# QK-norm and rotary in a hybrid decoder step: norm weights folded into the rotation matrix, one root and one reciprocal for all 16 tiles, spread back by a matmul

## The reference, cut to what matters

```
def rmsnorm(x, g):
    y = x * lax.rsqrt(jnp.mean(x * x, axis=-1, keepdims=True) + RMS_EPS)
    return y * g
def rope(x, pos):            # per half of 64 channels: x1, x2 of 32 each
    return concatenate([x1 * cos - x2 * sin, x2 * cos + x1 * sin])
q = rope(rmsnorm(q.reshape(bsz, t, H_ATT, 2, DH), W["q_norm"][e]), pos)
k = rope(rmsnorm(k.reshape(bsz, t, H_ATT, 2, DH), W["k_norm"][e]), pos)
```

## Time and profile before

| | |
|---|---|
| median of 3 runs | 3424.6 us |
| the profiled execution's own time | 3428.04 us |
| its span | 3426.4 us |
| PE, DVE, ACT busy share of the span | 94%, 44%, 32% |
| the stage at issue: last copy of the projection to first attention matmul | 452.24 to 522.73 us |

### The profile page before, as it was taken

How to read it: one execution, slowest core, us unless ns; L and a number is a source line. 1 busy time by engine, 2 the same in 40 slices (tenths; PEclk the granted TensorE clock), 3 DMA queues, 4 the chain that set the end, 5 groups by cost and what they waited for, 6 DMA issues and landing times.

```text
span 3426.4 us, 56080 instructions
## 1 busy us (share of the span) xinstructions
PE 3235.2 (94%) x21279; PEld 2959.4 (86%) x21279; DVE 1520.3 (44%) x1994; ACT 1083.0 (32%) x1287; POOL 29.7 (1%) x55
## 2 busy tenths in 40 slices
PE   7899987997789999999999989999989999999998
PEld 2588853775778998998998989999989999999998
DVE  1534574113653443443433564445554444444443
ACT  1322233103333323323323333333343333333332
POOL 0000000000000000000000000000000000000000
PEclk8999996877899999999999989999999999999999
DMA  9777777662347557557567534444434444444443
GB/s 347 243 246 249 236 267 261 226 239 80 100 146 247 179 179 245 177 184 246 167 193 243 161 114 150 151 147 149 148 116 149 151 147 148 151 147 149 151 147 110
DMA packets 512217, 624.17 MB, mean 182 GB/s; under 512 B 22416, under 2 KB 408081, under 8 KB 511444
## 3 DMA queue, kind: packets, MB, share of 16 engines
q1 hardware_dynamic: 504576, 595.68, 54.5%
q0 software_dynamic: 6112, 22.84, 1.8%
q10 hardware_dynamic: 1430, 4.24, 0.4%
HBM read 617.13 MB, written 5.54 MB: 182 GB/s over the span
## 4 chain that ended last, share of the span: by engine, by line
PE 88%; DVE 4%; DMA 4%; ACT 1%; issue 1%; SPq 0%; POOL 0%; POOLq 0%; DVEq 0%; ACTq 0%
PE mm L1417 80%; PE aux L1417 7%; DMA wide_first<-in_ada_mix_w 2%; DMA vpage<-in_cache_v 2%; PE mm L1510 1%; DVE a_rr L1201 1%; DVE l_g L1308 0%; SPq L362 0%; ACT tmp L613 0%; DVE a_qn L1204 0%; DVE pj L1212 0%; DVE p_s L1228 0%; DVE a_t L1210 0%; DVE rstd L898 0%; DVE a_t L1208 0%
## 5 line engine op out<-in xcount | busy, mean ns | idle before, releaser
L844 DVE TENSOR_TENSOR w_lo<-raw,w_hi 128x1024 fp32r<-128x1024 f32 x752 | 920.2, 1226 | 1431.2 <-ACT w_hi L526 1429.4
L526 ACT ACTIVATE w_hi<-raw 128x1024 fp32r<-128x1024 f32 x752 | 795.4, 1059 | 1724.8 <-PE mm L1417 1724.8
L1417 PE MATMUL mm<-h_hi,w_hi 128*128 128x320 f32 x3712 | 1164.6, 314 | 54.2 <-DVE h_lo L940 32.3
L1417 PE MATMUL mm<-h_hi,w_lo 128*128 128x320 f32 x3712 | 1151.4, 310 | 0.0
L1417 PE MATMUL mm<-h_lo,w_hi 128*128 128x320 f32 x3712 | 1151.3, 310 | 0.0
L1417 PEld LDWEIGHTS mm<-h_hi,w_hi 128*128 128x128 f32 x3712 | 701.5, 189 | 135.8 <-issue 133.2
L1417 PE MATMUL mm<-u_hi,w_hi 128*128 128x320 f32 x2304 | 712.0, 309 | 0.0
L1417 PE MATMUL mm<-u_hi,w_lo 128*128 128x320 f32 x2304 | 711.9, 309 | 0.0
L1417 PE MATMUL mm<-u_lo,w_hi 128*128 128x320 f32 x2304 | 711.9, 309 | 0.0
L1417 PEld LDWEIGHTS mm<-h_lo,w_hi 128*128 128x128 f32 x3712 | 701.7, 189 | 2.2 <-issue 2.2
L1417 PEld LDWEIGHTS mm<-h_hi,w_lo 128*128 128x128 f32 x3712 | 701.1, 189 | 0.0
(11 more groups left out here) (247 smaller groups left out, 1448.2 us busy)
## 6 DMA issues: line engine op xcount, KB each, us to landing
raw<-in_mlp_w SPq DMA_DIRECT2D x512, 512.0 KB, 3.6
narrow<-in_ada_mlp_w SPq DMA_DIRECT2D x256, 256.0 KB, 3.6
raw<-in_w_in_odd SPq DMA_DIRECT2D x96, 512.0 KB, 3.6
raw<-in_w_in_even SPq DMA_DIRECT2D x80, 512.0 KB, 6.6
wide_first<-in_ada_mix_w SPq DMA_DIRECT2D x64, 512.0 KB, 8.8
narrow<-in_ada_mix_w SPq DMA_DIRECT2D x128, 256.0 KB, 3.7
wide_later<-in_ada_mlp_w SPq DMA_DIRECT2D x64, 512.0 KB, 6.0
wide_later<-in_ada_mix_w SPq DMA_DIRECT2D x64, 512.0 KB, 5.2
```

Source lines behind the costliest of these rows:

```text
L526: fn(w_hi[:, slot], raw[:, slot], ACT.Copy).then_inc(hi_ready, 1)
L844: v.tensor_tensor(w_lo[:, slot], raw[:, slot], w_hi[:, slot].bitcast(F32), ALU.subtract).then_inc(lo_ready, 1)
L1417: return nc.tensor.matmul(out, lhsT, rhs, start=first, stop=last)
```

## The change

- The norm weight no longer multiplies the tile. VectorE first makes `rot_g`, the rotation matrix with each row scaled by the norm weight of k or of q (two instructions). TensorE turns the raw tile with it; VectorE multiplies the raw tile by weight and cos in one instruction, the turned tile by sin, and adds both into `pj`. These sums are not normed yet.
- The sums of squares are gathered in one PSUM bank. `sel` has 32 columns for each group of four tiles, so that tile i adds its two sums as rows 2(i // 4) and 2(i // 4)+1 of the strip i % 4 of `mm[:, 1, 0]`.
- After the 16 tiles there is one root and one reciprocal over that bank. A second loop spreads each tile's two rows over the 128 partitions by a matmul with 32 rows of `bsel`, and VectorE multiplies the tile by it.
- The adaLN chunks come one at a time in both loops, where they came in pairs; the transposes of v lie in the first loop, those of k in the second, and two folds in each.
- The table of constants is 120 columns wider in sum; the mask of the sample attention is one window of 120 columns.

```diff
@@ -50,9 +50,9 @@
-for _name, _cols in (("ident", 128), ("halves", 128), ("rot", 128), ("ones", 128), ("comb", 64), ("fold", NC),
+for _name, _cols in (("ident", 128), ("sel", 128), ("bsel", 512), ("rot", 128), ("ones", 128), ("comb", 64), ("fold", NC),
-                     ("mask_s", NB * TS)):
+                     ("mask_s", 120)):
...
@@ -67,7 +67,14 @@
-    put("halves", (p[:, None] // DH == p[None, :] // DH))
+    sel = np.zeros((P, 4, 32))
+    bsel = np.zeros((P, 4, P))
+    for q in range(4):
+        for n in range(2):
+            sel[DH * n:DH * n + DH, q, 2 * q + n] = 1.0
+            bsel[2 * q + n::32, q, DH * n:DH * n + DH] = 1.0
+    put("sel", sel.reshape(P, 128))
+    put("bsel", bsel.reshape(P, 512))
...
@@ -95,11 +102,8 @@
-    t = np.arange(TS)
-    mask = np.full((NB, P, TS), NEG)
-    for b in range(NB):
-        mask[b] = np.where((t[None, :] // DS == b) & (t[None, :] % DS <= q % 8), 0.0, NEG)
-    put("mask_s", mask.transpose(1, 0, 2).reshape(P, NB * TS))
+    t = np.arange(120)[None, :] - 56
+    put("mask_s", np.where((t >= 0) & (t < DS) & (t <= q % 8), 0.0, NEG))
...
@@ -222,9 +226,9 @@
-        a_rt = at("a_rt", RH + 24576 + 2560, [P, 2, T])
-        a_rr = at("a_rr", RH + 24576 + 5120, [P, 2, T])
-        a_qn = at("a_qn", RH + 24576 + 7680, [P, 2, T])
+        a_rt = at("a_rt", RH + 24576 + 2560, [P, T])
+        a_rr = at("a_rr", RH + 24576 + 3840, [P, T])
+        rot_g = at("rot_g", RH + 24576 + 5120, [P, 2, P])
...
@@ -683,27 +688,29 @@
                     split(2)
             rounds(1)
             act.wait_ge(pair_free, 22)
-            for i in range(17):
-
-                if i < 16:
-                    if i >= 2:
-                        act.wait_ge(qk_ms, i - 1)
-                    fn(a_sq[:, i % 2], pj[:, qk_tile(i), :], ACT.Square).then_inc(qk_sq, 1)
-                if i >= 1:
-                    act.wait_ge(qk_ms, i)
-                    if i >= 3:
-                        act.wait_ge(qk_norm, i - 2)
-                    fn(a_rt[:, (i - 1) % 2], mm[:, 1, (i - 1) % 2, 0:T], ACT.Sqrt, scale=1.0 / DH, bias=C("eps")
-                       ).then_inc(qk_root, 1)
-                if i != 8:
-
-                    n = i if i < 8 else i - 1
-                    tok, cols = (vtok, ktok)[n // 8], slice((n % 8) * P, (n % 8) * P + P)
-                    act.wait_ge(tok_t, n + 1)
-                    fn(tok[:, 0:2, cols], tok_bank(n)[:, 0:2 * P].rearrange("p (a f) -> p a f", a=2), ACT.Copy)
-                    fn(tok[0:TS, 2, cols], tok_bank(n)[0:TS, 2 * P:3 * P], ACT.Copy).then_inc(tok_ready, 1)
-                if i % 4 == 3:
+            def tok_out(n):
+
+                tok, cols = (vtok, ktok)[n // 8], slice((n % 8) * P, (n % 8) * P + P)
+                act.wait_ge(tok_t, n + 1)
+                fn(tok[:, 0:2, cols], tok_bank(n)[:, 0:2 * P].rearrange("p (a f) -> p a f", a=2), ACT.Copy)
+                fn(tok[0:TS, 2, cols], tok_bank(n)[0:TS, 2 * P:3 * P], ACT.Copy).then_inc(tok_ready, 1)
+
+            for i in range(16):
+                if i >= 2:
+                    act.wait_ge(qk_ms, i - 1)
+                fn(a_sq[:, i % 2], pj[:, qk_tile(i), :], ACT.Square).then_inc(qk_sq, 1)
+                if i < 8:
+                    tok_out(i)
+                if i == 8:
                     ada_out(True)
+            act.wait_ge(qk_ms, 16)
+            fn(a_rt[:, :], mm[:, 1, 0, 0:T], ACT.Sqrt, scale=1.0 / DH, bias=C("eps")).then_inc(qk_root, 1)
+            ada_out(True)
+            for n in range(8, 16):
+                tok_out(n)
+                if n == 14:
+                    ada_out(True)
+            ada_out(True)
             for h in range(H + 1):
 
                 if h < H:
@@ -1196,28 +1203,30 @@
             dve.wait_ge(pair_free, G.now)
 
 
-            def qk_normed(i):
-                dve.wait_ge(qk_root, i + 1)
-                step(v.reciprocal(a_rr[:, i % 2], a_rt[:, i % 2]))
-                settle()
+            step(v.tensor_scalar(rot_g[:, 0], C("rot"), V("k_norm"), None, ALU.mult))
+            v.tensor_scalar(rot_g[:, 1], C("rot"), V("q_norm"), None, ALU.mult).then_inc(qk_gain, 1)
+            for i in range(16):
                 g = V("k_norm") if i < 8 else V("q_norm")
-                v.scalar_tensor_tensor(a_qn[:, i % 2], pj[:, qk_tile(i), :], g, a_rr[:, i % 2], ALU.mult, ALU.mult).then_inc(qk_norm, 1)
-
-            def qk_turned(i):
-                dve.wait_ge(qk_norm, i + 1)
-                step(v.tensor_tensor(a_t1[:, i % 2], a_qn[:, i % 2], C("cos"), ALU.mult))
+                x = pj[:, qk_tile(i), :]
+                step(v.scalar_tensor_tensor(a_t1[:, i % 2], x, g, C("cos"), ALU.mult, ALU.mult))
                 dve.wait_ge(qk_rot, i + 1)
                 step(v.tensor_tensor(a_t2[:, i % 2], mm[:, 0, i % 2, 0:T], C("sin"), ALU.mult))
                 settle()
-                v.tensor_tensor(pj[:, qk_tile(i), :], a_t1[:, i % 2], a_t2[:, i % 2], ALU.add).then_inc(qk_ready, 1)
-
-            for i in range(17):
-                if i < 16:
-                    qk_normed(i)
-                if i >= 1:
-                    qk_turned(i - 1)
-                if i % 4 == 0 and i:
-                    ada_bias(1, 3 + i // 4)
+                dve.wait_ge(qk_sq, i + 1)
+                v.tensor_tensor(x, a_t1[:, i % 2], a_t2[:, i % 2], ALU.add).then_inc(qk_part, 1)
+                if i == 9:
+                    ada_bias(1, 4)
+            dve.wait_ge(qk_root, 1)
+            v.reciprocal(a_rr[:, :], a_rt[:, :]).then_inc(qk_inv, 1)
+            ada_bias(1, 5)
+            dve.wait_ge(qk_part, 16)
+            for i in range(16):
+                x = pj[:, qk_tile(i), :]
+                dve.wait_ge(qk_spread, i + 1)
+                v.tensor_tensor(x, x, mm[:, 0, i % 2, 0:T], ALU.mult).then_inc(qk_ready, 1)
+                if i == 9:
+                    ada_bias(1, 6)
+            ada_bias(1, 7)
 
 
             def p_scores(h):
...
@@ -1280,7 +1289,7 @@
-                c0 = COL["mask_s"][0] + TS * b
+                c0 = COL["mask_s"][0] + 56 - DS * b
...
@@ -1556,31 +1565,43 @@
                 turn_with_ada(h_hi, h_lo)
             pairs(2, h_hi, h_lo)
             pe.wait_ge(pair_free, 22)
-            for i in range(17):
-
-                if i < 16:
-                    pe.wait_ge(qk_sq, i + 1)
-                    if i >= 2:
-                        pe.wait_ge(qk_root, i - 1)
-                    mul(mm[:, 1, i % 2, 0:T], C("halves"), a_sq[:, i % 2], True, True).then_inc(qk_ms, 1)
-                if i != 8:
-
-                    n = i if i < 8 else i - 1
-                    if n >= 8:
-                        pe.wait_ge(qk_ready, n - 8 + 1)
-                    if n >= 2:
-                        pe.wait_ge(tok_ready, n - 1)
-                    tile = 16 + n if n < 8 else n
-                    for tt in range(3):
-                        rows = P if tt < 2 else TS
-                        ins = turn(tok_bank(n)[0:rows, P * tt:P * tt + P], pj[:, tile, P * tt:P * tt + rows])
-                    ins.then_inc(tok_t, 1)
-                if i < 16:
-                    ada(wide_later, range(2 * (i % 4), 2 * (i % 4) + 2))
-                if i >= 1:
-                    pe.wait_ge(qk_norm, i)
-                    mul(mm[:, 0, (i - 1) % 2, 0:T], C("rot"), a_qn[:, (i - 1) % 2], True, True).then_inc(qk_rot, 1)
-                if i < 16 and i % 4 == 3:
+            def tok_turn(n, tile):
+
+                if n >= 2:
+                    pe.wait_ge(tok_ready, n - 1)
+                for tt in range(3):
+                    rows = P if tt < 2 else TS
+                    ins = turn(tok_bank(n)[0:rows, P * tt:P * tt + P], pj[:, tile, P * tt:P * tt + rows])
+                ins.then_inc(tok_t, 1)
+
+            pe.wait_ge(qk_gain, 1)
+            for i in range(16):
+                strip = slice(32 * (i % 4), 32 * (i % 4) + 32)
+                if i >= 2:
+                    pe.wait_ge(qk_part, i - 1)
+                mul(mm[:, 0, i % 2, 0:T], rot_g[:, i // 8], pj[:, qk_tile(i), :], True, True).then_inc(qk_rot, 1)
+                if i < 8:
+                    tok_turn(i, 16 + i)
+                ada(wide_later, range(i % 8, i % 8 + 1))
+                pe.wait_ge(qk_sq, i + 1)
+                mul(mm[strip, 1, 0, 0:T], C("sel")[:, 32 * (i // 4):32 * (i // 4) + 32], a_sq[:, i % 2], i < 4, i >= 12
+                    ).then_inc(qk_ms, 1)
+                if i % 8 == 7:
+                    fold()
+            pe.wait_ge(qk_part, 16)
+            for i in range(16):
+                strip = slice(32 * (i % 4), 32 * (i % 4) + 32)
+                ada(wide_later, range(i % 8, i % 8 + 1))
+                if i == 0:
+                    pe.wait_ge(qk_inv, 1)
+                if i >= 2:
+                    pe.wait_ge(qk_ready, i - 1)
+                mul(mm[:, 0, i % 2, 0:T], const[strip, COL["bsel"][0] + P * (i // 4):COL["bsel"][0] + P * (i // 4) + P],
+                    a_rr[strip, :], True, True).then_inc(qk_spread, 1)
```

(7 more changed lines are left out.)

## The result

The changed kernel takes 3445.86 us (median of 5 runs, 3440.29 to 3456.51) against 3424.6 (3421.71 to 3429.55): 1.0066 of the time before, 95% interval 1.0044 to 1.0087. Run again beside later experiments it took 3439.95 against 3426.13, 1.0048 (1.0025 to 1.0071). The prediction was 3430, range 3421 to 3438. The direction was right and the size was wrong, 21 us in place of 5. The profiled execution took 3440.29 us with a span of 3438.6, the shortest of the five.

The account below looks back on a forecast made before the run. VectorE was taken to bound the stage before, TensorE after. Attention starting 5.3 us later, less 0.6 for clock, plus 0.2 for constants, gave +4.9: 3429.5 from 3424.6, raised to 3430 for half clock; range 3421 to 3438.

Parts of the forecast that it names:

- The bound before and after: Query/key norm stage: VectorE binds before at 3.98 us a step, TensorE at 2.73; afterwards TensorE binds.
- chunk alone: Both loops on TensorE: a single adaLN chunk costs 0.98 us, against 1.12 for a pair.
- step 2.05 or 2.58: First loop, steps 1 to 7 on TensorE: 2.05 us, or 0.54 more when the sum of squares finds its strip taken.
- bridge: Between the two loops: last sum, root, then fold and a chunk before the first spread, 3.1 us, 1.3 of it TensorE idle.
- spread: Second loop: the new 32-row matmul for each tile costs 0.76 us, bounds 0.1 and 0.87.
- wait before the fold: Second loop, fold 7: TensorE waits about 1.2 us for that step's token copies and `ares` on ScalarE.
- The splitting: First loop: 32 steps of one chunk take 31.4 us against 17.9 in pairs, adding 13.5 us.
- rival B: Slower clock: half-clock stretches at the idle gaps cost TensorE 1.6 us each; four give +6.5, 3436; chance 0.26.
- the half microsecond that the forecast has for half clock: Whole stage: a little added for possible half clock, taking 3429.5 to 3430.
- The change of tile: TensorE in both loops: changing tiling mode drains the engine, 0.11 us a change, so a spread can't lie beside a chunk.
- Rival A: Both loops: small tiles run side by side, spread and sum of squares cost at most 0.1; 12.6 less, 3417; chance 0.08.
- The attention's start at full clock: First 16 rows of the attention, 3.09 us at half clock before, should start at full clock: -0.6 us.

Follow-up runs that it names:

- the split pairs: Kernel before with ScalarE's Abs_reciprocal_sqrt replacing root and VectorE reciprocal, its chunk pairs also split around sum of squares and transposes: 3426.62 us, ratio 1.0006.
- the kernel with pairs: Changed kernel with the adaLN chunks of the second loop in pairs, in every second step: 3426.92 us, ratio 0.9998.
- the first execution: First profiled execution of the changed kernel itself, nothing else altered: 3440.29 us, the shortest of its five.
- the kernel with full rows and pairs: Changed kernel with the spread over all 128 rows (wrong factors) and chunks in pairs in both loops: 3410.72 us, ratio 0.9956.
- one word on ScalarE: Kernel before with ScalarE's Sqrt replaced by Abs_reciprocal_sqrt and VectorE's 16 reciprocals removed: 3409.52 us, ratio 0.9948.

## Why the prediction was wrong in its size

- *The bound before and after.* Right: VectorE bound the stage, TensorE lay at 2.7 us a step under it (2.60 when it was uncovered, since the pair costs 1.00 and not the 1.12 that I read), and VectorE, ScalarE and the transfers are not the bound after.
- *TensorE's unit costs.* Right to 0.1 us: chunk alone 0.98, step 2.05 or 2.58 (then 1.72 or 2.25), bridge 3.2, spread 0.73, wait before the fold 1.20. The splitting, 13.5 us on paper, is 15.4 with the pair at 1.00, and 17 with its changes of tile, as the split pairs show; the sum of the forecast has only chunks alone in it and does not change by this. Forecast from the copy of the projection to the scores: 75.8 us. Measured 89.9 (455.23 to 545.15).
- *The step that failed* is the price of rival B, and with it the half microsecond that the forecast has for half clock. I took stretches of half clock of 5 us with 1.6 lost in each, four of them at most, because the one inside the stage of before had ended soon; the 16 us at half clock in the attention's start, which stand in my own rows, did not enter the price. In the second loop a stretch doesn't end: 30.7, 71.7, 61.4 and 44.4 us in four executions with 32-row spreads, each ending only in the attention. From 517.18 to the scores the profiled execution took 28.0 us. At full clock it is 2.19 + 6 x 1.72 + 0.98 + 1.81 = 15.3 (1.81 from the last spread to the scores, 531.44 to 533.25 with 64 rows), so 12.7 were lost there. Another 1.6 went at the first chunk, at half clock after the wait for its transfer (459.53 to 464.71 is 5.2 us, and 3.5 with 64 rows, at full clock). Together that is 14.3, against the 14.1 between forecast and measurement. When the clock falls at the bridge the loss is 10 us more, and beyond the top of my range.
- *Why it doesn't end*: because of the 32 rows of the spread, as far as the variants show. With 128 rows and the same chunks the clock came back after 3.4 us and 19 to 25 us were gone from the median; with 64 rows, which change the tile as often, it came back after 6.8. I had written that the steps were fuller than those of before. In busy time they are, 30.0 of 30 us.
- *The clock's rule.* The Trainium skill ("TensorE: Matmul & The Clock Gate", Part 1) says that idle time lowers the clock and that busy time brings it back. The trace agrees with the first in so far as each fall in the second loop came behind a wait of 1.2 us and a fold. It does not agree with the second: TensorE was busy for 30.0 of 30 us at half clock.
- *The change of tile.* The Trainium skill ("TensorEngine Tiling (Array Packing)", Key Properties) says that a change of tiling mode drains the engine. The trace agrees: no spread starts inside a chunk (497.89 to 498.87 is the whole 0.98). Between two chunks a spread costs 0.73 or 0.74, with 32, 64 or 128 rows. Rival A's tiles side by side came only where two spreads followed each other, in the kernel with pairs.
- *The attention's start at full clock*, -0.6, did not come: its first 16 rows took 3.09 us, as before.
- *The late start.* The projection's last copy came 3.0 us later than before (455.23). In seven profiled executions with the wider constants it lies between 453.3 and 455.3, in four without them between 452.2 and 454.8. The 0.2 us of the constants can't be told from that.
- *What starts the fall* stays open. It came behind the bridge in four profiled executions (496.2 to 498.9 us) and at or behind the fold of step 7 in three (517.6, 519.4 and 514.6; the one at 519.4 had fallen at the bridge too). The same wait of 1.2 us with its fold stood without a fall at the bridge of the first execution and of the kernel with 64 rows, and at both places in the kernel with full rows and pairs. In the first execution the steps with 32-row spreads ran at full clock from 499 to 517. No run took the bridge's idle time away.

## What to carry to other kernels

Price an operation that moves onto the bound engine by its place: two matmuls that run side by side in strips cost 0.02 to 0.14 us as the second half of a pair and 0.98 when they stand alone. When work is added to TensorE that uses few rows of the array, look at the granted clock in the windows, because an engine that is busy all the time can stay at 1.2 GHz for as long as such steps last. Before a slow instruction is shared between tiles at the cost of matmuls, look for a function that makes it unnecessary: one word on ScalarE gave 19 us here, where the rebuilding took 21.

## What was not expected of the hardware

- A pair of chunks costs what one costs: 1.86 and 1.85 us at half clock, 1.00 and 0.98 at full clock.
- With TensorE busy 30.0 of 30 us the granted clock stayed at 0.50. From 517 to 533 us it was 0.52 with 32 rows in the spread, 0.86 with 64 and 0.89 with 128.
- Two spreads of 32 rows in different strips take what one takes when they follow each other: 1.37 us and 1.36 at half clock.
- A sum of squares in a strip that the chunk doesn't use is free: the step takes 2.05 us with it, what rotation, transposes and chunk take alone.
